# First attention: residual additions at the head of the vector engine's step; tails: loads released by the sync engine and the last normalisation step in halves

## What is computed

```
h = x
h = layer_norm(ALPHA * h + diff_attention(h))      # 8 heads, 4 query blocks of 128
h = layer_norm(ALPHA * h + hier_moe(h))            # 32 experts, 2 per token, width 512
h = layer_norm(ALPHA * h + pool_mixer(h))
h = layer_norm(ALPHA * h + hier_moe(h))
h = h + concat(forgetting_attention, rg_lru)(rmsnorm(h)) @ w_out
h = h + hierarchical_moe(rmsnorm(h))               # 32 experts, 2 per token, width 256
out = rmsnorm(h)
```

## Time and profile before

| | |
|---|---|
| median of 3 runs | 2207.31 us (2206.63 to 2207.64) |
| the profiled execution's own time | 2207.31 us |
| its span, first to last instruction | 2205.4 us |
| mean granted TensorE clock, share of full speed | 0.964 |
| PE busy | 2012.4 us, 91% |
| DVE busy | 673.9 us, 31% |
| ACT busy | 404.6 us, 18% |
| POOL busy | 120.7 us, 5% |
| DMA, mean over the span | 277 GB/s |

### The profile page before, as it was taken

One profiled execution on the slowest core, in us unless ns is written; L12 is line 12 of the kernel. 1 busy time (PEld: TensorE's weight loads), 2 busy tenths in 40 slices (PEclk: granted clock), 3 DMA queues, 4 the chain that ended last, 5 costly groups with the idle time before them and its releaser, 6 DMA issues.

```text
span 2205.4 us, 25848 instructions
## 1 busy us (share of the span) xinstructions
PE 2012.4 (91%) x10093; PEld 1067.4 (48%) x10093; DVE 673.9 (31%) x1584; ACT 404.6 (18%) x873; POOL 120.7 (5%) x148
## 2 busy tenths in 40 slices
PE   8999878999999999599999999999599989988873
PEld 4444434654554554554554554554454445644442
DVE  0154526411111111534411111111637224612113
ACT  1033413111111111121211111111223222112112
POOL 0000000100000000000100000000010001301100
PEclk9999988999999999799999999999799999999997
DMA  9931101699999999821699999999821110699995
GB/s 314 304 132 39 39 0 61 228 419 421 420 420 421 421 420 411 302 82 55 225 419 420 421 421 421 421 421 407 299 82 39 39 38 23 212 381 420 420 420 233
DMA packets 134625, 611.43 MB, mean 277 GB/s; under 512 B 15087, under 2 KB 53375, under 8 KB 71583
## 3 DMA queue, kind: packets, MB, share of 16 engines
q1 hardware_dynamic: 120735, 579.07, 66.3%
q0 software_dynamic: 13824, 31.48, 4.2%
HBM read 574.53 MB, written 48.55 MB: 283 GB/s over the span
## 4 chain that ended last, share of the span: by engine, by line
PE 82%; DMA 7%; DVE 6%; ACT 2%; issue 1%; POOL 0%; SPq 0%; POOLq 0%; ACTq 0%; DVEq 0%
PE bank L817 20%; PE bank L844 12%; PE bank L802 12%; PE bank L562 10%; DMA ring<-in_w_up_dram 5%; PE bank L702 4%; PE bank L574 4%; PE bank L548 3%; PE bank L826 3%; PE bank L656 2%; PE bank L1002 1%; PE bank L793 1%; PE bank L963 1%; PE bank L616 1%; PE bank L629 1%
## 5 line engine op out<-in xcount | busy, mean ns | idle before, releaser
L817 PE MATMUL bank<-ring,work 128*64 128x512 f32 x2048 | 450.7, 592 | 0.6 <-ACT work L1123 0.6
L1598 DVE TENSOR_TENSOR work<-work,bank 64x512 f32<-64x512 f32 (+1 forms) x96 | 87.0, 907 | 790.5 <-ACT work L1133 790.4
L844 PE MATMUL bank<-ring,work 128*64 128x512 f32 x1280 | 297.5, 603 | 3.6
L817 PEld LDWEIGHTS bank<-ring,work 128*64 128x64 f32 x2048 | 146.4, 137 | 291.6 <-issue 290.7
L802 PEld LDWEIGHTS bank<-work 128*128 128x128 f32 x2112 | 245.7, 191 | 57.1 <-issue 52.7
L802 PE MATMUL bank<-work 128*128 128x128 f32 x2112 | 270.8, 281 | 0.0
L562 PE MATMUL bank<-hT,ring 128*128 128x512 f32 x512 | 237.1, 606 | 0.7 <-ACT work L1065 0.7
L1138 ACT ACTIVATE work<-bank 64x512 f32<-64x512 f32 x96 | 56.7, 590 | 608.4 <-PE bank L844 608.4
L844 PEld LDWEIGHTS bank<-ring,work 128*64 128x64 f32 x1280 | 83.4, 137 | 146.1 <-issue 128.8
L562 PEld LDWEIGHTS bank<-hT,ring 128*128 128x128 f32 x512 | 94.0, 194 | 109.5 <-issue 107.6
L1133 ACT ACTIVATE work<-bank 64x512 f32<-64x512 f32 (+1 forms) x96 | 49.8, 518 | 441.6 <-PE bank L817 356.0
(11 more groups left out here) (291 smaller groups left out, 1747.7 us busy)
## 6 DMA issues: line engine op xcount, KB each, us to landing
ring<-in_moe_w_gate_dram SPq DMA_DIRECT2D x128, 1024.0 KB, 15.3
ring<-in_moe_w_up_dram SPq DMA_DIRECT2D x128, 1024.0 KB, 17.2
ring<-in_moe_w_down_dram SPq DMA_DIRECT2D x128, 1024.0 KB, 15.3
ring<-in_w_gate_dram SPq DMA_DIRECT2D x32, 1024.0 KB, 19.8
ring<-in_w_up_dram SPq DMA_DIRECT2D x32, 1024.0 KB, 21.9
ring<-in_w_down_dram SPq DMA_DIRECT2D x32, 1024.0 KB, 21.6
x_rows<-zeros SPq DMA_DIRECT2D x1, 12800.0 KB, 62.1
ring<-in_attn_w_qkv_dram SPq DMA_DIRECT2D x12, 1024.0 KB, 13.7
```

What stands on the lines that cost most here:

```text
L817: mm = pe.matmul(GU[BLK * a:BLK * a + BLK, :], xT_[:, 4 * kk + k, :], v[:, k, :], start=(kk + k == 0), stop=(kk + k == 4))
L844: mm = pe.matmul(DN[BLK * n:BLK * n + BLK, :], hT_[:, 2 * kk + k, :], v[:, k, 512 * n:512 * n + 512], start=(kk + k == 0), stop=(2 * kk + ...
L1598: dve.tensor_tensor(dealt(hg[:, 0:F], F // P), as_dealt(sg[:, 0:F], F // P), as_dealt(GU[BLK:P, 0:F], F // P), ALU.mult).then_inc(b.hg, 1)
```

## The change

Four edits.

1. In the first attention DVE's `add_heads(i)` moves from the end of step i + 33 to the head of step i + 32, ahead of `maxima`.
2. In the three tails POOL no longer waits for the stores: it reads the count and increments `over_moved` as soon as the last store is issued. SP waits for `over_moved` and then itself for both `y_stored` counts. If there were overflow blocks, POOL would wait for the stores inside the branch.
3. The last instruction of `tile_normal` and of `tile_rms` becomes two of 128x512, each with its own increment. PE's transposes of "ffn0" and "rms0" wait for each half; the final store becomes eight of 256 KB.
4. After the first two mixtures, the first row's addition of tile 1 moves behind the normalisation of tile 0.

```
             for step in range(5 * 8):
+                if step >= 32:
+                    add_heads(step - 32)
                 if step >= 8:
                     maxima(step - 8)
...
-                if step >= 33:
-                    add_heads(step - 33)
-            add_heads(7)
```

```
+            def load_tiles(l):
+
+                sp.wait_ge(over_moved, l + 1)
+                for y_stored in steps.y_stored:
+                    sp.wait_ge(y_stored, 16 * (E // 4) * (l + 1))
+                for tt in range(T):
+                    rows = y_rows[2 * P * tt:2 * P * tt + 2 * P, :].rearrange("(p k) d -> p (k d)", k=2)
+                    sp.dma_start(ytile[tt], rows).then_inc(routing.gathered[tt], 16)
...
-            for tt in range(T):
-                sp.wait_ge(out_ready, tt + 1)
-                sp.dma_start(t["out"][0, P * tt:P * tt + P, :], hn[:, tt, :]).then_inc(out_done, 16)
+                for n in range(2):
+                    c = slice(512 * n, 512 * n + 512)
+                    sp.wait_ge(out_ready, 2 * tt + n + 1)
+                    sp.dma_start(t["out"][0, P * tt:P * tt + P, c], hn[:, tt, c]).then_inc(out_done, 16)
...
-                for s in range(2):
-                    pool.wait_ge(main.y_stored[s], main.store0 + 16 * E // 4)
                 count = pool.value_load(ovi[0:1, 16:17], min_val=0, max_val=OVF)
                 with pool.If(count > 0):
+                    for s in range(2):
+                        pool.wait_ge(main.y_stored[s], main.store0 + 16 * E // 4)
...
-                pool.sem_inc(y_landed, 1)
+                pool.sem_inc(over_moved, 1)
```

```
                 for tt in tiles:
...
                     for kk in range(chunks // 4):
+                        if name in ("ffn0", "rms0"):
+                            pe.wait_ge(tiles_written, s.src0 + 2 * tt + kk + 1)
...
-                dve.scalar_tensor_tensor(out=h[:, tt, :], in0=h[:, tt, :], scalar=rstd[:, tt:tt + 1],
-                                         in1=lnp[:, D:2 * D], op0=ALU.mult, op1=ALU.add).then_inc(done, 1)
-                dve.wait_ge(done, count0 + tt + 1)
+                for n in range(2):
+                    hs = h[:, tt, 512 * n:512 * n + 512]
+                    dve.scalar_tensor_tensor(out=hs, in0=hs, scalar=rstd[:, tt:tt + 1],
+                                             in1=lnp[:, D + 512 * n:D + 512 * n + 512], op0=ALU.mult, op1=ALU.add)\
+                        .then_inc(done, 1)
+                dve.wait_ge(done, count0 + 2 * tt + 2)
...
             for tt in range(T):
-                if tt + 1 < T:
+                if 1 <= tt < T - 1:
                     combine_tile(0, tt + 1, 0)
                 tile_normal(tt, 1, tiles_written, turns["ffn0"].src0)
                 if tt + 1 < T:
+                    if tt == 0:
+                        combine_tile(0, 1, 0)
                     combine_tile(0, tt + 1, 1)
                     tile_variance(tt + 1)
```

More of the change, by code:

```diff
@@ L137, in program @@
         slots_dealt, slots_loaded, slots_turned = sem("slots_dealt"), sem("slots_loaded"), sem("slots_turned")
-        slots_known, y_landed = sem("slots_known"), sem("y_landed")
+        slots_known, over_moved = sem("slots_known"), sem("over_moved")
         rows_zeroed, x_dealt = sem("rows_zeroed"), sem("x_dealt")
@@ L156, in program @@
             src0, copied0 = written, copied
-            written += T if name != "x" else 0
+            written += {"x": 0, "ffn0": 2 * T, "rms0": 2 * T}.get(name, T)
             copied += T * chunks // 4
@@ L523, in _ @@
             mixture(2)
-            sp.wait_ge(y_landed, 3)
+            load_tiles(2)
             for tt in range(T):
-                load_tile(tt)
-            for tt in range(T):
-                sp.wait_ge(out_ready, tt + 1)
-                sp.dma_start(t["out"][0, P * tt:P * tt + P, :], hn[:, tt, :]).then_inc(out_done, 16)
-            sp.wait_ge(out_done, 16 * T)
+                for n in range(2):
+                    c = slice(512 * n, 512 * n + 512)
+                    sp.wait_ge(out_ready, 2 * tt + n + 1)
+                    sp.dma_start(t["out"][0, P * tt:P * tt + P, c], hn[:, tt, c]).then_inc(out_done, 16)
+            sp.wait_ge(out_done, 32 * T)
         @block.tensor
@@ L586, in turn @@
                         pe.wait_ge(x_loaded[tt], 16)
-                    else:
+                    elif name not in ("ffn0", "rms0"):
                         pe.wait_ge(tiles_written, s.src0 + tt + 1)
                     for kk in range(chunks // 4):
+                        if name in ("ffn0", "rms0"):
+                            pe.wait_ge(tiles_written, s.src0 + 2 * tt + kk + 1)
                         for k in range(4):
@@ L1177, in _ @@
             for tt in range(T):
-                act.wait_ge(ln3_done, tt + 1)
+                act.wait_ge(ln3_done, 2 * tt + 2)
                 tile_square(tt)
@@ L1299, in tile_rms @@
                 dve.wait_ge(par_sem, 16)
-                dve.scalar_tensor_tensor(out=dst[:, tt, :], in0=h[:, tt, :], scalar=r, in1=gain,
-                                         op0=ALU.mult, op1=ALU.mult).then_inc(done, 1)
+                for n in range(2):
+                    c = slice(512 * n, 512 * n + 512)
+                    dve.scalar_tensor_tensor(out=dst[:, tt, c], in0=h[:, tt, c], scalar=r, in1=gain[:, c],
+                                             op0=ALU.mult, op1=ALU.mult).then_inc(done, 1)
             dve.memset(zeros[:, :], 0.0).then_inc(zero_ready, 1)
@@ L1677, in _ @@
                 if tt + 1 < T:
+                    if tt == 0:
+                        combine_tile(1, 1, 0)
                     combine_tile(1, tt + 1, 1)
@@ L1895, in _ @@
             bcast(rms0_gain, t["mix_norm_2"], par.rms0, D)
-            pool.wait_ge(ln3_done, T)
+            pool.wait_ge(ln3_done, 2 * T)
             def vector(dst, src, s):
```

6 lines of the change are left out of this document (1 added, 5 removed).

## The result

| | median us | runs | range us |
|---|---|---|---|
| before | 2206.97 | 4 | 2206.52 to 2207.64 |
| changed | 2174.96 | 4 | 2173.1 to 2180.7 |

The ratio is 0.9859, with a 95% interval of 0.984 to 0.9878: 1.4% faster. The profiled execution is the slowest of the four, 2180.7 us with a span of 2178.8. Over all launches that follow the kernel before spread from 2200.3 to 2211.1 us (44 runs, median 2206.6), the changed one from 2172.35 to 2180.7 (8 runs, median 2174.4): 32 us between the medians, where 28.9 were forecast.

The account below looks back on a forecast made before the run. PE was taken as the bound, idling in the first attention at a lowered clock, plus three serial tails. Savings of 25.5, 3.1 and 0.25 make 28.9 us: 2207.3 - 28.9 = 2178.4 us, range 2175.5 to 2181.5.

Parts of the forecast that it names:

- likeliest case: Whole kernel: the forecast itself, 2178.4 us, given a chance of 0.72.
- The waits go, 38.74 us for the steps: First attention, steps 33 to 39: PE's six waits, 14.7 us, vanish; the stretch takes 38.74 us against 64.22.
- part 1: Moved additions in the first attention: 25.5 us less, 14.7 from waits and 10.8 from the clock staying at 1.00.
- 0, within 1 us either way for the clock's phase: Stretch behind the first attention's loop: length unchanged, within 1 us either way.
- Part 2: Release of the loads in the three tails: gaps from store landing to load issue shrink, gain 3.1 us.
- First tail: Behind the first mixture: PE starts 0.35 us later; an earlier half of tile 0 is of no use.
- Second tail: Behind the second mixture: root costs 0.35 us, first half is out 0.64 us earlier; 0.3 us gained.
- Third tail: Last store, 256 KB in place of 512 KB: 0.3 us less, bounds 0 and 1.0.
- Halving "nothing": DVE's split instructions: two halves take 1.29 us against 1.28 whole, cost taken as 0; upper bound 0.6 for seven.
- the lost clock: Rivals in the first attention: clock low in part, 2183.8 us, chance 0.13; low altogether, 2189.2 us, chance 0.04.
- the addition takes the wait's place: Rival, first attention: combine comes too late for PE's transposes, each step one chain; about 2213 us, chance 0.02.
- The tails' rival: Three tails: the release gains nothing, exposed root and halves cost their bounds; 2183.1 us, chance 0.06.

Follow-up runs that it names:

- a3: The changed kernel with the additions put back at the end of the step, so the tail edits alone; median 2201.39 us.
- a4: The kernel before with SP waiting for the stores itself and nothing else changed; median 2202.40 us.
- c3: The changed kernel with three dummy DVE instructions behind each addition at the head of steps 32 to 39; 2181.45 us in one run.
- b1: The changed kernel, with POOL issuing the second tail's gain broadcast only when all four loads have landed; median 2176.10 us.
- c0: The changed kernel, with POOL issuing the second tail's gain broadcast when the first load has landed; median 2175.67 us.
- c1: The changed kernel with copies before the next root (two tails), second-tail normalisation before the next tile's second addition, gain broadcast behind the first load; median 2167.49 us.
- b3: The changed kernel with the first row's addition of tile 1 put back ahead of the normalisation of tile 0; median 2172.63 us.
- b4: The changed kernel, with ACT copying each transposed tile ahead of the next tile's root in the first tail; median 2165.87 us.
- a1: The changed kernel launched again without any change, as yardstick; median 2173.85 us.

## Why the prediction was right, and where it was not

The sign, the size and the likeliest case were right: 2178.4 forecast, 2174.96 measured, in the range and 3.4 us below the point. By its steps:

- **The waits go, 38.74 us for the steps.** Right: 38.42, at a clock of 1.00 as taken from 200 to 230 us. The addition was to delay combine "by at most that", 0.69: it delays it by 0.05 at most, since it runs while PE computes the scores that DVE needs next. PE "asks" 6.80 us after the scores: 6.92, because the scores of the next step, 0.43 us up to its transposes, were left out, while the two terms taken, from starts to ends, were 0.31 too long (2.96 and 3.53 from start to start). Slack 1.74 us at the widest step, where 0.94 was forecast.
- **25.5 us for part 1.** Nearly right for the steps, 25.8 us against before and 27.2 to 27.3 against a3 and a4. With the stretch behind the loop it is 27.2 to 29.8 us against the three profiles with late additions. "0, within 1 us either way for the clock's phase" behind the loop was the mis-sized term: 77.75 before, 73.8 to 74.7 with the new order (c3's dummies aside), but 74.4 with the old one in other executions. It is the clock's and belongs to no edit, but a forecast from one profile carries it as an error of some 3 us.
- **Part 2, "Gain 3.1 us".** The step that failed. The gaps shrank as said, 3.23 to 0.26. But "Behind SP's wait ... stand only weight loads" looked at SP's queue and not at POOL's, the engine that was set free: its broadcast overtook the loads, and in the nine profiles where it did the first load landed in 5.3 to 7.4 us in place of 4.8 to 4.9. b1, c0 and c1 show it by taking it away (4.75 to 4.94). And in the first tail the last store landed in 3.2 to 3.7 us in all twelve profiles with the new release, in 2.7 in both without. Why was not tried; in the third tail, with the same release, it landed in 2.65 us as before. SP's wake-up, taken as 0.05, was 0.07 to 0.10. Of 3.1 some 1.0 us arrived (0.7 - 0.6 + 0.9) in the stages; a4's total fell by more, 4 us, and the stages don't explain that.
- **First tail, "0.35 us more".** 0.48: 0.34 of them the bare root (b3), 0.13 the half. That the earlier half is of no use because of ACT's order was right, and b4 shows what that order costs: 5.7 us with the clock by the stages, the largest thing left in the tails.
- **Second tail, 0.3 us gained.** 0.06: the half gives 0.41 and not 0.64, since two splits on its chain cost 0.13 each.
- **Third tail, 0.3 with bounds of 0 and 1.0.** 0.2 against a whole store that lands in 2.7 us, 1.1 against one of 3.6. The store of 256 KB takes 2.08 us where the whole takes 2.65, 0.57 less. The Trainium skill, "DMA: Bandwidth & Descriptors", section "Anatomy of one DMA", gave 0.6 by a fit that it states for DMAs issued by GpSimd; SyncE issues these, and the trace agrees even so. The rest went into the four halved steps on the way, some 0.13 each.
- **Halving "nothing".** Wrong: 744 to 753 ns each, 1.41 to 1.42 us a pair against 1.28. The row was read at another operation (`TENSOR_TENSOR` of L1742), whose pace does not hold for this one. The Trainium skill, "VectorE: DVE Perf Modes", section "The TRN2 errata — SBUF-src ops pay a fixed extra latency per instruction", gave about 0.16, by a formula that it states for `tensor_tensor`: nearer than the row, 0.13 measured. Seven of them: 0.9 us.

Of the rivals the lost clock did not come, and "the addition takes the wait's place" was further off than thought: c3 needed 2.1 us more in each step to bring one wait of 0.82. The tails' rival came in part. The mechanism of part 1, most of the sum, was right. That the sum came out so close is partly luck, since two errors had opposite signs: by the stages part 1 with the stretch behind it gave 1.7 to 4.3 us more than forecast, and the tails 0.75 to 1.65 us in place of 3.4.

## What to carry to other kernels

When a wait is taken from an engine, read what it does next, its DMAs above all: here a broadcast that had always waited its turn went ahead of the loads on the critical path and took back what the release gave; it belongs behind the first load, and not behind all of them. When a producer is split or hurried, look first whether the consumer's helper is free: ACT's copies behind the next tile's root cost 4.2 us of idle PE and about 1.5 more at the lower clock behind it. And time single stages of an untouched stretch in a second execution before reading a few us out of one profile, with the stretch behind them, which may give the difference back.

## What the runs showed of the hardware

Stretches whose instructions are the same repeat to 0.01 us where the granted clock is 1.00 (99.97 to 99.99 us from the 216th to the 525th matmul in all 14 profiles), and lie up to 5 us apart where it dips (158.8 to 164.1 us for the 495 matmuls ahead of the 376 above, and 74.3 to 79.4 us for these). A shorter wait ahead of work at the lower level can give more than its own length: with 4.24 us less (b4 against a1) the granted clock rose 2.9 us behind the first of the 64 matmuls and not 5.9, and they took 1.45 us less. A 4 MB load in four parts whose first is needed at once landed that part in 4.7 to 5.0 us alone. Behind a broadcast of 512 KB it took 6.2 to 7.4 us where that was issued 1.7 to 2.0 us before the load, and 5.3 to 6.2 where it was 2.6 to 2.7 us.
